# Order of the products inside a weight chunk: all products with the high part first, then those with the low part

## The chip, the cores and the metric

The kernel runs on one core of a Trainium2 chip (trn2). The metric is the device time of one execution in microseconds (us). It was run three times before the change; the median is 1704.13 us, the runs lie between 1700.52 and 1705.7. Of this kernel a difference of about 0.3% can be told from none.

## The reference

One inference step of a hybrid decoder layer (depth 1, model width 2048) for a prompt of 256 tokens and eight samples of one token each. The 264 tokens share the weights. Cut to what matters:

```python
z = x @ w_in                                   # 2048 x 13316, split among the mixers and four gates
A: forgetting attention, B: S5 state space, C: HGRN2, D: spatial-gating MLP      # four branches, 512 wide
m = sum_k sigmoid(gate_k) * (branch_k @ w_branch[k])
x = LN(alpha * x + m @ w_out)
gate, up = split(x @ w_ffn_up)                 # 2048 x 2*5632
x = LN(alpha * x + (silu(gate) * up) @ w_ffn_down)
```

Branch B needs, per group, an input matrix of 16 channels times 64 complex states. It is built from the parameters, transposed on TensorE and then used as the left operand for the state inputs. All outputs are fp32, with caches and states beside the two y tensors.

## The kernel before, in words

**A product of two fp32 numbers in three.** All big products are done in the type fp32r. To keep the precision of fp32, both operands are split into a high and a low part: `high = round(x)`, `low = x - high`. A product is then high weight times high operand, high weight times low operand and low weight times high operand, three matmuls that add up in PSUM. The right operand is 264 columns wide (256 prompt tokens and 8 samples; in the first four steps of the up projection 266). The output of one weight tile is 128 x 264 and lies in one PSUM bank.

**Chunks.** Weights come in chunks of 512 KB, 128 x 1024 numbers, that is eight tiles of 128 x 128: four k tiles (`kk`) times two column halves (`half`), and 24 products. Two halves go to two PSUM banks, and a pass of several chunks adds up in the same two. There are 540 chunks: 276 for w_in, w_branch, the S5 GLU and w_out (`chunk(n)`, L816 to L818) and 264 for the feed-forward layer (`products`, L1177 to L1179; the last chunk of all has a form of its own, `last_products`). In the feed-forward part the up projection has 22 steps of 8 chunks, of which the first four (with 266 columns) and the fifth are written out and the others are a hardware loop; the down projection has 8 passes of 11 chunks, written out.

**Who does what with a chunk.** SP loads it into a ring (five slots, later four). ACT writes its high part (`hi_done` or `hi2` goes up by one; L1290, L1586), DVE subtracts and writes the low part (`lo_done` or `lo2`; L1702, L2395), TensorE multiplies. DVE waits for ACT's high part, and TensorE waits for DVE's low part before the first of the 24 products. With the last product TensorE raises `used` (or `used2`), and by that ACT may write the slot again, SP may load it, and ACT or DVE may evacuate a finished pass.

**The order on TensorE.** The order of the work is written out by hand. `until(n)` issues all chunks up to number n, and the small products of the branches stand between such calls. Every engine runs its list in order and waits for semaphores only. ACT and DVE have lists of their own (`weights(n)`, `more()`), in which splits of chunks and the small work of the branches are interleaved.

**S5's matrix.** DVE builds `bd` in the middle of its first splits (L1888 to L1892) and then tells `s5_bd`; GpSimd builds the identity. TensorE transposes `bd` into banks 4 and 5 (`transposes("s5_bt", r, ...)`, L832, two times four). ACT copies the result into `bt` (L1364) and tells `s5_bt_ready`, for which TensorE waits after chunk 13 before the samples' products (L970). 

**Other places that come up.** L954 is a warm-up of six matmuls on a tile of ones ahead of the first chunk. Between chunks 54 and 62 L1021 broadcasts the values of one sample after each chunk, and DVE updates that sample's state from it (L2070). L839 sums over partitions with a matrix of ones (fp32). `hp` holds the operand of the down projection: for each k tile 264 high numbers, then 264 low ones 288 places further on; `x1p` holds that of the up projection in the same way.

Of the kernel before, what the change touches and what calls it, by code (L numbers as in the profile page):

```python
# [12 lines left out]
P = 128  # L13
# [4 lines left out]
TOK = SEQ + DEC  # L18
# [12 lines left out]
CK = 4  # L31
# [200 lines left out]
def trunk(nc, A, O):  # L232
# [551 lines left out]
    def _(pe):  # L784
        done = [FIRST]

        def chunk(n):
# [15 lines left out]
            if kind == "out":  # L803
                right_h, right_l = mh, ml
                if a == 0:
                    pe.wait_ge(sem("ml_done"), 2 * kc + 2)
            pe.wait_ge(sem("lo_done"), n - FIRST + 1)
            slot, tiles = n % RING, 1 if kind == "ff" else 2
            per = CK * 2 // tiles
            for kk in range(per):  # L810
                k = kc * per + kk
                first, last = k == 0, k == count * per - 1
                for half in range(tiles):
                    out = PS[:, BANK(p) + half, 0:TOK]
                    c = slice((kk * tiles + half) * P, (kk * tiles + half) * P + P)
                    nc.tensor.matmul(out, w_split[:, slot, 0, c], right_h[:, k, :], start=first, stop=False)  # L816
                    nc.tensor.matmul(out, w_split[:, slot, 0, c], right_l[:, k, :], start=False, stop=False)  # L817
                    ins = nc.tensor.matmul(out, w_split[:, slot, 1, c], right_h[:, k, :], start=False, stop=last)  # L818
            ins.then_inc(sem("used"), 1)

        def weights(upto):
# [131 lines left out]
        for _ in range(6):  # L953
            nc.tensor.matmul(PS[:, 7, :].rearrange("p (a t) -> p a t", a=4), ones[:, :],  # L954
                             ones[:, :].unsqueeze(1).to_broadcast([P, 4, P]), start=True, stop=True)
        until(11)
        pe.wait_ge(*told("ident_ready", 1))
        pe.wait_ge(*told("s5_bd", 1))
        for r in range(2):
# [207 lines left out]

        def products(slot, bank, right_h, right_l, k0, first, last, width=TOK):  # L1170

            for kk in range(CK):
                rh, rl = right_h(k0 + kk, width), right_l(k0 + kk, width)
                for half in range(2):
                    out = PS[:, bank + half, 0:width]
                    c = slice((kk * 2 + half) * P, (kk * 2 + half) * P + P)
                    nc.tensor.matmul(out, w_hi[:, slot, c], rh, start=(first and kk == 0), stop=False)  # L1177
                    nc.tensor.matmul(out, w_hi[:, slot, c], rl, start=False, stop=False)  # L1178
                    ins = nc.tensor.matmul(out, w_lo[:, slot, c], rh, start=False, stop=(last and kk == CK - 1))  # L1179
            ins.then_inc(sem("used2"), 1)  # L1180

# [24 lines left out]
        def up_chunk(i, j, right_h, right_l, width=TOK):  # L1206
            n, p, kc = C_UP + j, P_UP + j // 4, j % 4
            if kc == 0:
                pe.wait_ge(sem(f"evac{p % 2}"), i + p // 2)
            pe.wait_ge(sem("lo2"), i * 8 + (n + 1))  # L1210
            products(n % RING2, BANK(p), right_h, right_l, CK * kc, kc == 0, kc == 3, width)

        for i in range(Z_STEPS):
            for j in range(8):
# [16 lines left out]
        for m in range(8):  # L1231
            p = P_DOWN + m
            for kc in range(DOWN_CHUNKS):
                n = C_DOWN + m * DOWN_CHUNKS + kc
                if kc == 0:
                    pe.wait_ge(sem(f"evac{p % 2}"), p // 2)
                if m == 0:
                    pe.wait_ge(sem("hl_done"), CK * (kc + 1) // 2)
                pe.wait_ge(sem("lo2"), n + 1)
                if (m, kc) == (7, DOWN_CHUNKS - 1):  # L1240
                    last_products(n % RING2, BANK(p), h_high, h_low, CK * kc)
                else:
                    products(n % RING2, BANK(p), h_high, h_low, CK * kc, kc == 0, kc == DOWN_CHUNKS - 1)
                if (m, kc) == (4, 5):
                    layer_pivot(1)

# [1410 lines left out]
```

## Time and profile before

| what | before |
|---|---|
| median of three runs | 1704.13 us (1700.52 to 1705.7) |
| the profiled execution, its span | 1702.31 us, 1700.4 us |
| TensorE busy | 1689.7 us, 99% of the span, 13806 matmuls |
| weight loads busy | 1642.0 us, 97%, 13806 |
| DVE, ACT, GpSimd busy | 1076.0 us (63%), 798.1 us (47%), 142.3 us (8%) |
| granted TensorE clock, mean | 0.997 |

The span runs from the first to the last instruction of the profiled execution; the time of an execution has a little more around it. Each engine's busy time is a share of the span. Matmuls overlap in the profile, because one takes 280 ns or so from its start to its end and the next starts some 120 ns after it; a busy share of 99% therefore says that TensorE always had a product under way, and the distance between two starts says how fast it is.

### The profile page before, as it was taken

To read this page: it belongs to the slowest core of one execution; us is meant where nothing else is said; L and a number is where in the kernel's file an instruction comes from. 1 tells how busy PE (TensorE), PEld (TensorE's weight loads), DVE (VectorE), ACT (ScalarE), POOL (GpSimd) and SP (SyncE) were. 2 spreads that over 40 slices of the span, in tenths; PEclk is the share of its full clock that TensorE was granted. 3 is DMA by queue.
4 is the path that set the end of the run, shared out by engine and by line. 5 is a ranking of instruction groups with operands and counts; after the bars stand their busy time and mean duration, and the time that the engine had idled before them with its cause. 6 is when DMAs were issued, how large, how long until landed. Compare 5 with 4: busy or idle time off the path is not lost.

```text
span 1700.4 us, 33405 instructions
## 1 busy us (share of the span) xinstructions
PE 1689.7 (99%) x13806; PEld 1642.0 (97%) x13806; DVE 1076.0 (63%) x1275; ACT 798.1 (47%) x894; POOL 142.3 (8%) x148
## 2 busy tenths in 40 slices
PE   9999999999999999999999999999999999999998
PEld 8999998999999999999999999999999999999997
DVE  7888897766557666455688784444444444455655
ACT  5655544656444444444355563444434443333433
POOL 8200000000012555000000000000000000000000
PEclk9999999999999999999999999999999999999998
DMA  8566567776657888666556556656556565655652
GB/s 259 160 208 165 159 216 246 229 233 212 211 149 241 287 255 251 190 185 179 181 175 197 186 166 194 185 181 179 183 185 182 178 183 186 186 177 170 197 176 76
DMA packets 310582, 329.75 MB, mean 194 GB/s; under 512 B 12223, under 2 KB 292035, under 8 KB 310212
## 3 DMA queue, kind: packets, MB, share of 16 engines
q1 hardware_dynamic: 309068, 326.59, 62.7%
q8 instruction: 84, 1.38, 0.3%
q10 hardware_dynamic: 1400, 1.54, 0.3%
q14 instruction: 30, 0.25, 0.0%
HBM read 322.31 MB, written 5.77 MB: 193 GB/s over the span
## 4 chain that ended last, share of the span: by engine, by line
PE 98%; DVE 1%; DMA 0%; issue 0%; ACT 0%; SPq 0%; DVEq 0%
PE ps L816 16%; PE ps L817 16%; PE ps L818 16%; PE ps L1178 15%; PE ps L1177 15%; PE ps L1179 15%; PE ps L889 1%; PE ps L1066 1%; PE ps L924 1%; PE ps L854 0%; PE ps L832 0%; DMA w_in_ring<-in_w_in 0%; DVE w_split L1702 0%; PE ps L839 0%; PE ps L1269 0%; PE ps L867 0%
## 5 line engine op out<-in xcount | busy, mean ns | idle before, releaser
L2395 DVE TENSOR_TENSOR w_lo<-w_raw,w_hi 128x1024 fp32r<-128x1024 f32 x264 | 322.8, 1225 | 318.8 <-ACT w_hi L1586 315.8
L1702 DVE TENSOR_TENSOR w_split<-w_in_ring,w_split 128x1024 fp32r<-128x1024 f32 x276 | 351.2, 1276 | 234.3 <-ACT w_split L1290 224.3
L816 PE MATMUL ps<-xh,w_split 128*128 128x264 f32 x1680 | 481.2, 286 | 2.1 <-DVE w_split L1702 2.1
L1586 ACT ACTIVATE w_hi<-w_raw 128x1024 fp32r<-128x1024 f32 x264 | 279.8, 1061 | 429.8 <-PE ps L1179 425.0
L817 PE MATMUL ps<-xl,w_split 128*128 128x264 f32 x1680 | 477.9, 284 | 0.0
L818 PE MATMUL ps<-xh,w_split 128*128 128x264 f32 x1680 | 476.5, 284 | 0.0
L1290 ACT ACTIVATE w_split<-w_in_ring 128x1024 fp32r<-128x1024 f32 x276 | 291.2, 1059 | 352.1 <-DMA w_in_ring<-in_w_in 263.8
L1178 PE MATMUL ps<-x1p,w_hi 128*128 128x264 f32 (+1 forms) x1408 | 400.3, 284 | 0.0
L1177 PE MATMUL ps<-x1p,w_hi 128*128 128x264 f32 (+1 forms) x1408 | 399.0, 283 | 0.0
L1179 PE MATMUL ps<-x1p,w_lo 128*128 128x264 f32 (+1 forms) x1408 | 393.9, 280 | 0.0
L816 PEld LDWEIGHTS ps<-xh,w_split 128*128 128x128 f32 x1680 | 315.9, 188 | 18.1 <-issue 12.7
L817 PEld LDWEIGHTS ps<-xl,w_split 128*128 128x128 f32 x1680 | 315.9, 188 | 0.2
L818 PEld LDWEIGHTS ps<-xh,w_split 128*128 128x128 f32 x1680 | 315.9, 188 | 0.0
L1177 PEld LDWEIGHTS ps<-x1p,w_hi 128*128 128x128 f32 x1408 | 265.1, 188 | 0.0
L1179 PEld LDWEIGHTS ps<-x1p,w_lo 128*128 128x128 f32 x1408 | 265.0, 188 | 0.0
L1178 PEld LDWEIGHTS ps<-x1p,w_hi 128*128 128x128 f32 x1408 | 264.3, 188 | 0.0
L1178 PE MATMUL ps<-hp,w_hi 128*128 128x264 f32 x696 | 197.7, 284 | 0.0
L1177 PE MATMUL ps<-hp,w_hi 128*128 128x264 f32 x696 | 196.9, 283 | 0.0
L1179 PE MATMUL ps<-hp,w_lo 128*128 128x264 f32 x696 | 195.8, 281 | 0.0
L1177 PEld LDWEIGHTS ps<-hp,w_hi 128*128 128x128 f32 x696 | 130.9, 188 | 0.0
L1179 PEld LDWEIGHTS ps<-hp,w_lo 128*128 128x128 f32 x696 | 130.8, 188 | 0.0
L1178 PEld LDWEIGHTS ps<-hp,w_hi 128*128 128x128 f32 x696 | 130.7, 188 | 0.0
(499 smaller groups left out, 1787.6 us busy)
## 6 DMA issues: line engine op xcount, KB each, us to landing
w_in_ring<-in_w_in SPq DMA_DIRECT2D x210, 512.0 KB, 3.8
w_raw<-in_w_ffn_up SPq DMA_DIRECT2D x176, 512.0 KB, 4.1
w_raw<-in_w_ffn_down SPq DMA_DIRECT2D x88, 512.0 KB, 3.5
kv<-in_cache_k SPq DMA_DIRECT2D x64, 258.0 KB, 3.8
w_in_ring<-in_w_branch SPq DMA_DIRECT2D x32, 512.0 KB, 4.5
kv<-in_cache_v SPq DMA_DIRECT2D x64, 256.0 KB, 3.7
w_in_ring<-in_w_out SPq DMA_DIRECT2D x32, 512.0 KB, 3.4
x_t<-in_x SPq DMA_DIRECT2D x8, 264.0 KB, 7.0
```

Of the source, the lines that this page charges most:

```text
L816: nc.tensor.matmul(out, w_split[:, slot, 0, c], right_h[:, k, :], start=first, stop=False)
L817: nc.tensor.matmul(out, w_split[:, slot, 0, c], right_l[:, k, :], start=False, stop=False)
L818: ins = nc.tensor.matmul(out, w_split[:, slot, 1, c], right_h[:, k, :], start=False, stop=last)
L889: ins = nc.tensor.matmul(PS[32 * h:32 * h + DEC, bank, :].rearrange("p (a t) -> p a t", a=4), q_rows[:, h, b, :], kv[:, u % 2, :, h * P:h ...
L924: ins = nc.tensor.matmul(PS[32 * j:32 * j + 32, bank, :], ptt[:, 32 * (8 * b + 4 * half + j):32 * (8 * b + 4 * half + j) + 32], kv[:, u % ...
L1177: nc.tensor.matmul(out, w_hi[:, slot, c], rh, start=(first and kk == 0), stop=False)
L1178: nc.tensor.matmul(out, w_hi[:, slot, c], rl, start=False, stop=False)
L1179: ins = nc.tensor.matmul(out, w_lo[:, slot, c], rh, start=False, stop=(last and kk == CK - 1))
L1290: A_(w_split[:, n % RING, 0, :], w_in_ring[:, n % RING, 1, :], ACT.Copy).then_inc(sem("hi_done"), 1)
L1586: A_(w_hi[:, n % RING2, :], raw[:, n % RING2, :], ACT.Copy).then_inc(sem("hi2"), 1)
L1702: V.tensor_tensor(w_split[:, slot, 1, :], w_in_ring[:, slot, 1, :], w_split[:, slot, 0, :], ALU.subtract).then_inc(sem("lo_done"), 1)
L2395: V.tensor_tensor(w_lo[:, n % RING2, :], raw[:, n % RING2, :], w_hi[:, n % RING2, :], ALU.subtract).then_inc(sem("lo2"), 1)
```

## The change

Within a chunk the 24 products keep their operands, their banks and their number. Before, the three products of a weight tile came one after another. After, the 16 products with the high weights of all eight tiles come first, tile by tile (high operand, low operand), and then the eight with the low weights. TensorE waits for the high part before the 16 and for the low part before the eight. The first product of a pass starts its bank and the last low product ends it. The last chunk of all keeps its order and its wait. And the transposes of S5's matrix move from behind chunk 11 to behind chunk 12.

```diff
@@ chunk(n)
-            pe.wait_ge(sem("lo_done"), n - FIRST + 1)
+            pe.wait_ge(sem("hi_done"), n - FIRST + 1)
             for kk in range(per):
                 k = kc * per + kk
                 for half in range(tiles):
...
                     nc.tensor.matmul(out, w_split[:, slot, 0, c], right_h[:, k, :], start=(k == 0), stop=False)
                     nc.tensor.matmul(out, w_split[:, slot, 0, c], right_l[:, k, :], start=False, stop=False)
-                    ins = nc.tensor.matmul(out, w_split[:, slot, 1, c], right_h[:, k, :], start=False, stop=last)
+            pe.wait_ge(sem("lo_done"), n - FIRST + 1)
+            for kk in range(per):
+                k = kc * per + kk
+                for half in range(tiles):
...
+                    ins = nc.tensor.matmul(out, w_split[:, slot, 1, c], right_h[:, k, :], start=False,
+                                           stop=(k == count * per - 1))
             ins.then_inc(sem("used"), 1)
@@ before the transposes of s5_bt
-        until(11)
+        until(12)
@@ products(): the same, with the count of the chunk as an argument
+            pe.wait_ge(sem("hi2"), count)
             for kk in range(CK):
...
                     nc.tensor.matmul(out, w_hi[:, slot, c], rh, start=(first and kk == 0), stop=False)
                     nc.tensor.matmul(out, w_hi[:, slot, c], rl, start=False, stop=False)
+            pe.wait_ge(sem("lo2"), count)
+            for kk in range(CK):
+                rh = right_h(k0 + kk, width)
+                for half in range(2):
...
                     ins = nc.tensor.matmul(out, w_lo[:, slot, c], rh, start=False, stop=(last and kk == CK - 1))
             ins.then_inc(sem("used2"), 1)
@@ up_chunk, and the down loop in the same way; before last_products the wait for lo2 stays
-            pe.wait_ge(sem("lo2"), i * 8 + (n + 1))
-            products(n % RING2, BANK(p), right_h, right_l, CK * kc, kc == 0, kc == 3, width)
+            products(i * 8 + (n + 1), n % RING2, BANK(p), right_h, right_l, CK * kc, kc == 0, kc == 3, width)
```

## Rows read from the trace of the kernel before

**Rows 1.** Profile: busy us (share of span) xinstructions; last chain by engine.

```profile
PE 1689.7 (99%) x13806; PEld 1642.0 (97%) x13806; DVE 1076.0 (63%) x1275; ACT 798.1 (47%) x894; POOL 142.3 (8%) x148
...
PE 98%; DVE 1%; DMA 0%; issue 0%; ACT 0%; SPq 0%; DVEq 0%
```

**Rows 2.** Waits of TensorE's matmuls: total us, times, longest us.

```profile
PE ps L816 <- DVE w_split L1702: 2.1, 2, 1.8
PE ps L954 <- POOLq L252: 1.1, 1, 1.1
```

**Rows 3.** Windows: stretch, length, busy (count) by engine, granted clock, DMA.

```profile
720.00:820.00 100.00, 100.00 (x826) 100.00 (x825) 54.95 (x55) 44.19 (x49) 0.00 (x0) 1.00 0.63 182
1020.00:1420.00 400.00, 400.00 (x3336) 400.00 (x3335) 193.47 (x174) 165.26 (x175) 0.00 (x0) 1.00 0.60 183
1460.00:1560.00 100.00, 100.00 (x836) 100.00 (x835) 52.36 (x51) 36.82 (x35) 0.00 (x0) 1.00 0.58 180
1580.00:1660.00 80.00, 80.00 (x661) 80.00 (x660) 46.74 (x47) 32.48 (x34) 0.00 (x0) 1.00 0.61 189
940.00:1000.00 60.00, 60.00 (x489) 60.00 (x488) 47.71 (x64) 32.24 (x43) 0.00 (x0) 1.00 0.58 178
860.00:920.00 60.00, 60.00 (x493) 60.00 (x492) 49.55 (x72) 32.68 (x51) 0.00 (x0) 1.00 0.58 185
```

**Rows 4.** Timeline of TensorE at 1568.7 us: start, us, instruction.

```profile
1568.86 0.61 PE L839 MATMUL ps<-acc_d,ones 128*128 128x264 f32 x2
```

**Rows 5.** Timeline of the first chunk's start; in brackets: idle, releaser.

```profile
7.96 1.02 PE L954 MATMUL ps<-ones 128*128 128x512 f32 x2
8.30 1.06 ACT L1290 ACTIVATE w_split<-w_in_ring 128x1024 fp32r<-128x1024 f32 x1 [3.20 <-DMA w_in_ring<-in_w_in]
9.39 1.22 DVE L1702 TENSOR_TENSOR w_split<-w_in_ring,w_split 128x1024 fp32r<-128x1024 f32 x1 [3.55 <-ACT w_split L1290]
...
10.76 0.36 PE L816 MATMUL ps<-xh,w_split 128*128 128x264 f32 x1 [1.78 <-DVE w_split L1702]
```

**Rows 6.** Timeline of weight loads and DVE's splits, 186 to 217 us.

```profile
186.41 0.19 PEld L1021 LDWEIGHTS ps<-t,pick 72*128 72x128 f32 x1
189.64 0.19 PEld L1021 LDWEIGHTS ps<-t,pick 72*128 72x128 f32 x1
192.80 0.19 PEld L1021 LDWEIGHTS ps<-t,pick 72*128 72x128 f32 x1
202.14 1.22 DVE L1702 TENSOR_TENSOR w_split<-w_in_ring,w_split 128x1024 fp32r<-128x1024 f32 x1
203.42 0.19 PEld L816 LDWEIGHTS ps<-xh,w_split 128*128 128x128 f32 x1 [0.21 <-DVE w_split L1702]
206.32 0.19 PEld L1021 LDWEIGHTS ps<-t,pick 72*128 72x128 f32 x1
215.37 1.22 DVE L1702 TENSOR_TENSOR w_split<-w_in_ring,w_split 128x1024 fp32r<-128x1024 f32 x1
216.44 0.19 PEld L818 LDWEIGHTS ps<-bh,w_split 128*128 128x128 f32 x1
216.71 0.19 PEld L816 LDWEIGHTS ps<-xh,w_split 128*128 128x128 f32 x1
```

**Rows 7.** Timeline around S5's transposes, 41 to 50 us.

```profile
41.37 0.87 DVE L1892 TENSOR_TENSOR bd<-tmp 64x256 f32<-64x256 f32 x2
41.71 1.06 ACT L1290 ACTIVATE w_split<-w_in_ring 128x1024 fp32r<-128x1024 f32 x1 [2.48 <-DMA w_in_ring<-in_w_in]
42.39 1.23 DVE L1702 TENSOR_TENSOR w_split<-w_in_ring,w_split 128x1024 fp32r<-128x1024 f32 x1 [0.15 <-DVE bd L1892]
42.95 1.03 PE L832 MATMUL ps<-ident,bd 128*128 128x128 f32 x8
48.14 1.31 ACT L1364 ACTIVATE bt<-ps 128x512 f32<-128x512 f32 x2
49.77 0.63 PE L970 MATMUL ps<-su,bt 32*128 32x8 f32 x16
```

More of the change, by code:

```diff
@@ L811, in chunk @@
                 k = kc * per + kk
-                first, last = k == 0, k == count * per - 1
                 for half in range(tiles):
@@ L815, in chunk @@
                     c = slice((kk * tiles + half) * P, (kk * tiles + half) * P + P)
-                    nc.tensor.matmul(out, w_split[:, slot, 0, c], right_h[:, k, :], start=first, stop=False)
+                    nc.tensor.matmul(out, w_split[:, slot, 0, c], right_h[:, k, :], start=(k == 0), stop=False)
                     nc.tensor.matmul(out, w_split[:, slot, 0, c], right_l[:, k, :], start=False, stop=False)
-                    ins = nc.tensor.matmul(out, w_split[:, slot, 1, c], right_h[:, k, :], start=False, stop=last)
+            pe.wait_ge(sem("lo_done"), n - FIRST + 1)
+            for kk in range(per):
+                k = kc * per + kk
+                for half in range(tiles):
+                    out = PS[:, BANK(p) + half, 0:TOK]
+                    c = slice((kk * tiles + half) * P, (kk * tiles + half) * P + P)
+                    ins = nc.tensor.matmul(out, w_split[:, slot, 1, c], right_h[:, k, :], start=False,
+                                           stop=(k == count * per - 1))
             ins.then_inc(sem("used"), 1)
@@ L1166, in _, with products @@
         until(END - 1)
-        def products(slot, bank, right_h, right_l, k0, first, last, width=TOK):
+        def products(count, slot, bank, right_h, right_l, k0, first, last, width=TOK):
+            pe.wait_ge(sem("hi2"), count)
             for kk in range(CK):
@@ L1178, in products @@
                     nc.tensor.matmul(out, w_hi[:, slot, c], rl, start=False, stop=False)
+            pe.wait_ge(sem("lo2"), count)
+            for kk in range(CK):
+                rh = right_h(k0 + kk, width)
+                for half in range(2):
+                    out = PS[:, bank + half, 0:width]
+                    c = slice((kk * 2 + half) * P, (kk * 2 + half) * P + P)
                     ins = nc.tensor.matmul(out, w_lo[:, slot, c], rh, start=False, stop=(last and kk == CK - 1))
@@ L1238, in _ @@
                     pe.wait_ge(sem("hl_done"), CK * (kc + 1) // 2)
-                pe.wait_ge(sem("lo2"), n + 1)
                 if (m, kc) == (7, DOWN_CHUNKS - 1):
+                    pe.wait_ge(sem("lo2"), n + 1)
                     last_products(n % RING2, BANK(p), h_high, h_low, CK * kc)
                 else:
-                    products(n % RING2, BANK(p), h_high, h_low, CK * kc, kc == 0, kc == DOWN_CHUNKS - 1)
+                    products(n + 1, n % RING2, BANK(p), h_high, h_low, CK * kc, kc == 0, kc == DOWN_CHUNKS - 1)
                 if (m, kc) == (4, 5):
```

## The prediction

> **What bounds the kernel now.** I read the head of the page first: the span is 1700.4 us, TensorE is busy for 99% of it, and 98% of the chain that ended last is its matmuls [rows 1]. The profiled execution took 1702.31 us, 1.9 more than its span; the median shown is 1704.13, so I work out a difference on the span and take it off the median. Next I read the list of waits: in the whole execution TensorE's matmuls waited for a low part (DVE, L1702) twice, 2.1 us in all, 1.8 of it before the first chunk, and they waited for no low part of the second ring [rows 2]. So the change moves waits on the right engine, but waits that hardly exist. Last I read windows over six stretches with nothing but weight products in them, because 540 chunks of 24 products are what TensorE's time is made of: what one product takes there is worth more than all waits together.
>
> **The pace of a product.** A window counts an instruction that it only cuts; matmuls of 0.28 us that follow each other every 0.12 add about 2.35. So 400 us with 3336 counted are 400/3333.65 = 120.0 ns for one product, in the up phase; 1460:1560 gives 120.0 in the first half of the down phase; 1580:1660 gives 80/658.65 = 121.5 in its second half; 720:820 gives 121.4 in the first weights; 860:920 gives 122.3 in the output projection; 940:1000 gives 123.3 in the first four up steps, where the right operand is two columns wider [rows 3]. The granted clock is 1.00 in all six, the level of 2.4 GHz, so the clock doesn't make the difference. Nor does the shape: the down phase runs 120.0 and then 121.5 with the same instructions on the same tile hp, and what stands between is one short interruption, the two fp32 sums of L839 [rows 4]. So this engine's pace isn't fixed by columns alone. It falls into one steady rhythm or another, and which one depends on what was read before. The change keeps every product and every operand but puts them in another order: a rhythm is what it can upset.
>
> **What goes: the start.** The first chunk's high part is ready at 8.30 + 1.06 = 9.36 us, the low part at 9.39 + 1.22 = 10.61, and the first product starts at 10.76, 0.15 later [rows 5]. After the change it waits for the high part only: 9.36 + 0.15 = 9.51. The low part is wanted after 16 products, 16 x 0.1214 = 1.94 us later, at 11.45, when it has long been there. Gain 1.25 us. The warm-up matmuls end at 7.96 + 1.02 = 8.98, so they aren't in the way.
>
> **What goes: the stretch where DVE is late.** Between 186 and 206 us DVE works off eight sample states between its splits. TensorE's L1021 (four of its seven rows are shown) stands behind each chunk there and comes seven times from 186.41 to 206.32: 19.91 us in six steps. The shortest step is 3.16 (189.64 to 192.80); six of them are 18.96, so 0.95 us were lost. At 216.44 the step to the next weight load is 0.27 in place of 0.12, 0.15 more [rows 6]. With the low part wanted 1.94 us later these go. But TensorE now comes 1.25 us earlier and DVE, busy with its own queue here, doesn't. The split that ends at 202.14 + 1.22 = 203.36 belongs to the chunk that started at 203.42; that chunk would now start at 203.42 - 1.25 - 0.95 = 201.22 and want it at 203.16: 0.20 late, 0.25 with the delay of a semaphore. The one that ends at 215.37 + 1.22 = 216.59 is wanted at about 216.71 - 1.25 - 0.95 - 0.15 + 0.25 + 1.94 = 216.55: 0.05 late, 0.1 with the delay. So 1.10 - 0.35 = 0.75 us stay.
>
> **What moves: the S5 transposes.** They need bd, which DVE finishes at 41.37 + 0.87 = 42.24. Before, they start at 42.95, after chunk 11. With TensorE 1.25 earlier they would come at 41.70 and wait 0.55; behind chunk 12, which takes 24 x 0.1214 = 2.91, they come at about 44.6 and don't. Chunk 12 itself then starts at 41.7 and wants its low part at 43.6; DVE finishes it at 42.39 + 1.23 = 43.62, just in time, at worst 0.15 late with the delay. The eight transposes issue no DMA and pass nothing but chunk 12 in TensorE's queue; SP and GpSimd wait for none of them. Their readers: ACT copies bt at 48.14, late for other reasons, and TensorE's L970 wants the copies (ready at 48.14 + 1.31 = 49.45) at 49.77 [rows 7]. TensorE comes there 1.25 earlier, at 48.5. ACT's queue up to that point hangs on a weight chunk at 41.71, for which it sat idle 2.48 us, and that transfer is issued when TensorE gives a slot back, so it moves with TensorE. I take 0. If ACT stays where it is, 1.0 of the 1.25 is lost here.
>
> **What is added.** One more wait in each of 539 chunks. Behind it stand the chunk's eight low products and then all that TensorE has queued; ACT (who reuses w_hi), SP (who reloads the slot) and the evacuations wait for the last of the eight, as before, and that is still the chunk's last product. A wait that is already met costs nothing that can be seen: in the 400 us of the up phase there are 139 of them and a product still takes 120.0 [rows 3]; the rounding of that pace, 0.04 ns a product, leaves 1 ns a chunk, 0.5 us in all, as the upper end. ACT's split takes 1.06 us and DVE's 1.22 [rows 5] of the 2.9 of a chunk; neither becomes the bound. The sum: -1.25 - 0.75 = -2.0 us. Its bounds are -2.4 (nothing is late) and +0.5 (DVE and ACT take all of it back, and the waits cost their upper end).
>
> **The pace after it.** No row shows the new order, so I bound it by the paces that the rows do show. A chunk had the right operands high, low, high for each weight tile; now it has high, low sixteen times in turn, then high eight times. How often a high follows a high, a low a high and a high a low is eight times a chunk in both orders, and every product still has its own weight load. That speaks for the same pace, and I take a change of 0. The bounds: 4656 products run at 120.0 now (3456 of the later up steps, 1200 of the first down chunks). At 121.5 they cost +7.0 us, at the 123.3 of the wider steps +15.4. Downwards, the 5856 products of the first weights at 120.0 in place of 121.4 to 121.5 give -8.5; the 768 of the output projection, the 768 wider ones and the 912 of the late down phase give -1.8, -2.5 and -1.4 more.
>
> The rows say that the same product takes 120.0 or 121.5 ns. The Trainium skill (SBUF — State Buffer, Who interferes with whom) gives TensorE two read ports of its own and says it waits for no one; and "TensorE: Matmul & The Clock Gate", Back-to-back issue gap, puts an isolated matmul at its columns over 2.4 GHz and 2.5 ns, which for 264 columns is 112.5 ns, an estimate from that page. By these the order can't matter to the pace, and the time is the sum of the waits alone; by the rows it can, since two stretches with one shape differ. The measurement decides, so the rivals below keep their chances.
>
> **The forecast and the rivals.** About 5 us, 0.3%, is what a measurement here can tell from no change: faster is under 1699.0, slower over 1709.2.
>
> *The waits go and the pace stays* (0.40): 1704.1 - 2.0 = 1702.1; its own range is 1699.5 to 1705.5. For it: the equal counts of neighbours; against it: the two paces of one tile.
>
> *The start is not kept* (0.05): ACT's copies of bt or DVE's states hand the lead back: 1703.5 to 1704.5.
>
> *The rhythm of the later phases is lost* (0.30), the one that ends on the other side. Place: the up steps from 1010 us and the first 50 down chunks, where a product takes 120.0. Eight high operands in a row, or the change from pairs to singles once a chunk, throw it into the rhythm that the second half of the down phase already has. Price 7.0 us, less 2.0: 1709.1; if the first weights also go to the 122.3 of the output projection, 0.9 x 5856 = 5.3 more, 1714. It decides for slower as soon as all 4656 lose 1.5 ns. For it: one interruption was enough to lose the rhythm for good [rows 4]. About 0.07 of the 0.30 stays within 0.3%.
>
> *The first weights find the rhythm* (0.25): high and low in strict turn is a simpler pattern than before. 1704.1 - 2.0 - 8.5 = 1693.6; with every slow stretch, 1688. Against it: four stretches out of six don't have it now. About 0.02 of this stays within 0.3%.
>
> So faster 0.23, same 0.40 + 0.05 + 0.07 + 0.02 = 0.54, slower 0.23. The range reaches from 1691 (most of the last case) to 1712 (most of the third).
>
> **What would show it.** The first product at 9.5 us; no PE wait for a low part in the list, or only ones of 0.3 around 203 and 216; L832 at 44 to 45 us with no idle before it, L970 at about 48.5. The windows in the same stretches tell the rest: 120.0 in the up phase keeps the forecast, 121.5 there makes it wrong to the slow side, and under 121 in the first weights makes it wrong to the fast side. A new TensorE wait for ACT's high parts would make it wrong in a way that I gave no chance.

## The result

The change makes the kernel faster: 1689.45 us (median of six runs, 1688.39 to 1691.82) against 1702.81 for the kernel before in the same session (six runs, 1700.11 to 1705.7). The ratio is 0.9927, its 95% interval 0.9916 to 0.9938. The forecast was 1702.1, "same" in the sense of within 0.3%, with a range down to 1691; all three were wrong. Of the runs reported below one, a tenth run of e2_in_only, took 6881.47 us and is left out of that kernel's interval.

The profiled execution of after took 1688.39 us with a span of 1686.6, 13.8 less than the span before. The lines of after that answer to [rows 1 to 7] follow; line numbers have moved (L954 is L960, L1021 is L1027, L1179 is L1192).

The head and the chain, as in [rows 1]. TensorE is the bound as before, and has 13.2 us less to do with the same 13806 instructions:

```profile
PE 1676.5 (99%) x13806; PEld 1630.5 (97%) x13806; DVE 1078.4 (64%) x1275; ACT 798.3 (47%) x894; POOL 142.2 (8%) x148
...
PE 97%; DMA 1%; POOL 1%; DVE 1%; ACT 0%; issue 0%; SPq 0%; DVEq 0%; POOLq 0%; ACTq 0%
```

All waits of TensorE's matmuls (total us, times, longest), as in [rows 2]. The wait for low parts is gone, and two new ones stand there:

```profile
PE ps L960 <- POOLq L252: 1.1, 1, 1.1
PE ps L815 <- ACT gate L1322: 0.8, 1, 0.8
PE ps L1151 <- DVEq L252: 0.7, 1, 0.7
```

The windows, as in [rows 3], cut to where each stage now lies. A count holds about 2.4 matmuls that the window only cuts, so the pace is the length over the count less 2.4:

```profile
720.00:800.00 80.00, 80.00 (x661) 80.00 (x660) 43.50 (x44) 35.66 (x39) 0.00 (x0) 1.00 0.63 179
1020.00:1400.00 380.00, 380.00 (x3214) 380.00 (x3213) 186.23 (x168) 159.24 (x167) 0.00 (x0) 1.00 0.60 186
1460.00:1550.00 90.00, 90.00 (x762) 90.00 (x762) 46.18 (x46) 33.96 (x32) 0.00 (x0) 1.00 0.57 183
1570.00:1650.00 80.00, 80.00 (x679) 80.00 (x678) 47.97 (x49) 33.45 (x34) 0.00 (x0) 1.00 0.61 194
940.00:1000.00 60.00, 60.00 (x488) 60.00 (x487) 47.70 (x65) 32.43 (x43) 0.00 (x0) 1.00 0.58 178
860.00:910.00 50.00, 50.00 (x412) 50.00 (x411) 40.38 (x58) 25.52 (x37) 0.00 (x0) 1.00 0.59 191
```

Here is the gain. In the up phase from step 4 on (second line) a product takes 380/3211.6 = 118.3 ns, where it took 120.0. Both halves of the down phase (third and fourth) run at 118.5 and 118.2, where they ran at 120.0 and 121.5; by the starts of the chunks both are at 118.3. The other three stand at 121.5, 123.6 and 122.1: within half a ns of before.

The matmul L845, which answers to [rows 4], still interrupts the down phase; now the same pace goes on behind it:

```profile
1559.72 0.61 PE L845 MATMUL ps<-acc_d,ones 128*128 128x264 f32 x2
```

The pace inside one chunk of the up phase (timeline of TensorE: start, us, instruction):

```profile
1200.92 1.12 PE L1192 MATMUL ps<-x1p,w_lo 128*128 128x264 f32 x8
1201.88 0.28 PE L1184 MATMUL ps<-x1p,w_hi 128*128 128x264 f32 x1
1202.00 0.28 PE L1185 MATMUL ps<-x1p,w_hi 128*128 128x264 f32 x1
1202.12 0.28 PE L1184 MATMUL ps<-x1p,w_hi 128*128 128x264 f32 x1
...
1203.76 0.64 PE L1192 MATMUL ps<-x1p,w_lo 128*128 128x264 f32 x4
```

The eight low products take 1201.88 - 1200.92 = 0.96 us, 120 ns each. The first two high ones take 0.24, 120 each. The other fourteen take 1.64 (1202.12 to 1203.76), 117. By the start times of all chunks of these steps, 15 of a chunk's 24 distances are at 116.7 on the mean, and a chunk takes 2840 ns where it took 2880.

The start, as in [rows 5], and the sample states, as in [rows 6] (first and last of seven weight loads):

```profile
7.34 1.06 ACT L1302 ACTIVATE w_split<-w_in_ring 128x1024 fp32r<-128x1024 f32 x1 [2.21 <-DMA w_in_ring<-in_w_in]
8.60 0.19 PEld L815 LDWEIGHTS ps<-xh,w_split 128*128 128x128 f32 x1 [0.24 <-issue]
8.63 0.69 PE L815 MATMUL ps<-xh,w_split 128*128 128x264 f32 x1
...
184.64 0.19 PEld L1027 LDWEIGHTS ps<-t,pick 72*128 72x128 f32 x1
...
203.56 0.19 PEld L1027 LDWEIGHTS ps<-t,pick 72*128 72x128 f32 x1
```

S5's transposes, as in [rows 7]:

```profile
40.76 0.87 DVE L1904 TENSOR_TENSOR bd<-tmp 64x256 f32<-64x256 f32 x2
44.14 1.04 PE L838 MATMUL ps<-ident,bd 128*128 128x128 f32 x8
45.68 1.31 ACT L1376 ACTIVATE bt<-ps 128x512 f32<-128x512 f32 x2
48.04 1.97 PE L976 MATMUL ps<-su,bt 32*128 32x8 f32 x64
```

Where the 13.8 us of span went, by the starts of the stages in the two traces: the first product starts 2.1 earlier (10.76 to 8.63), and of the lead 1.4 is left where up step 4 begins (1010.1 to 1008.7). Up steps 4 to 21 take 414.7 before and 409.0 after, the first 50 down chunks 144.25 and 142.25, the last 38 110.9 and 108.1: together 10.5. The tail behind the last product takes 20.4 before and 18.5 after: 1.9. That tail difference isn't the change's. Before, the engine's rows double in length at its end; after, they don't:

```profile
1687.76 1.15 PE L1269 MATMUL ps<-mu_r,minus 1*128 1x264 f32 x4
1688.84 2.13 PE L1266 MATMUL ps<-yp,ident 128*128 128x264 f32 x4
1690.90 2.12 PE L1269 MATMUL ps<-mu_r,minus 1*128 1x264 f32 x4
```

```profile
1676.91 1.16 PE L1278 MATMUL ps<-yp,ident 128*128 128x264 f32 x4
1678.00 1.15 PE L1281 MATMUL ps<-mu_r,minus 1*128 1x264 f32 x4
```

Windows of the two ends (the third number from the right is the granted clock) show the cause, before and then after:

```profile
1688.00:1700.30 12.30, 5.02 (x12) 2.76 (x11) 6.98 (x11) 6.37 (x13) 0.00 (x0) 0.53 0.50 176
```

```profile
1676.00:1686.50 10.50, 3.15 (x12) 1.83 (x12) 7.05 (x11) 6.32 (x13) 0.00 (x0) 0.64 0.58 206
```

Before, the clock is at its lower level, 1.2 GHz, while the last two rows run, and these take 2.13 us in place of 1.16; after, it falls only when they are done. When the clock falls differs between executions, in kernels with the change and without: with it the profiled tails run from 18.5 us (after, where the clock falls 11.0 behind the last product of the last chunk) to 22.5 (e7_low272, 6.5 behind it), without it they are 20.4 (before, 8.9 behind it) and 18.5 (e18_before_turn, 13.2 behind it).

### The profile page after: what moved, and what is told of

The parts are those of the page before. It is cut to its first block, busy times and chain, and to the rows that moved or that the text cites. A ratio compares the mean times of both kernels' runs of the same rounds, so it can differ in the third digit from the quotient of the medians.

```text
span 1686.6 us, 33405 instructions
## 1 busy us (share of the span) xinstructions
PE 1676.5 (99%) x13806; PEld 1630.5 (97%) x13806; DVE 1078.4 (64%) x1275; ACT 798.3 (47%) x894; POOL 142.2 (8%) x148
## 4 chain that ended last, share of the span: by engine, by line
PE 97%; DMA 1%; POOL 1%; DVE 1%; ACT 0%; issue 0%; SPq 0%; DVEq 0%; POOLq 0%; ACTq 0%
PE ps L815 15%; PE ps L823 15%; PE ps L1192 15%; PE ps L816 15%; PE ps L1185 15%; PE ps L1184 15%; PE ps L895 1%; PE ps L1072 1%; DMA w_in_ring<-in_w_in 1%; PE ps L860 1%; PE ps L960 0%; PE ps L838 0%; PE ps L930 0%; POOL v_sum L779 0%; PE ps L845 0%; PE ps L873 0%
## 5 line engine op out<-in xcount | busy, mean ns | idle before, releaser
L815 PE MATMUL ps<-xh,w_split 128*128 128x264 f32 x1680 | 421.7, 287 | 0.8 <-ACT gate L1322 0.8
L816 PE MATMUL ps<-xl,w_split 128*128 128x264 f32 x1680 | 416.3, 283 | 0.0
L1184 PE MATMUL ps<-x1p,w_hi 128*128 128x264 f32 (+1 forms) x1408 | 341.3, 280 | 0.0
L1185 PE MATMUL ps<-x1p,w_hi 128*128 128x264 f32 (+1 forms) x1408 | 340.6, 280 | 0.0
L815 PEld LDWEIGHTS ps<-xh,w_split 128*128 128x128 f32 x1680 | 315.9, 188 | 15.5 <-issue 12.7
L823 PE MATMUL ps<-xh,w_split 128*128 128x264 f32 x1680 | 238.8, 284 | 0.0
L823 PEld LDWEIGHTS ps<-xh,w_split 128*128 128x128 f32 x1680 | 218.2, 188 | 0.1
L1192 PE MATMUL ps<-x1p,w_lo 128*128 128x264 f32 (+1 forms) x1408 | 198.9, 283 | 0.0
L1192 PEld LDWEIGHTS ps<-x1p,w_lo 128*128 128x128 f32 x1408 | 181.6, 188 | 0.0
L1184 PE MATMUL ps<-hp,w_hi 128*128 128x264 f32 x696 | 167.4, 279 | 0.0
L1185 PE MATMUL ps<-hp,w_hi 128*128 128x264 f32 x696 | 166.8, 279 | 0.0
L1192 PE MATMUL ps<-hp,w_lo 128*128 128x264 f32 x696 | 97.8, 283 | 0.0
L1192 PEld LDWEIGHTS ps<-hp,w_lo 128*128 128x128 f32 x696 | 89.2, 188 | 0.0
```

## The experiments

One window, 1020 to 1400 us, lies inside up steps 4 to 21 in every kernel. It is shown for each; the pace is 380 us over the count less 2.4 (after: x3214, 118.3 ns). Kernels are compared by this pace first, because single times also differ by the tail: 18.5 us in after, 21.9 in e6_half_major and 22.0 in e17_cross_mended. Edits are shown against after, or against the kernel that the text names, and cut to the feed-forward where both parts of the kernel get the same.

### The change in parts

**e1_ff_only.** Only `products()` has the new order; `chunk()` and the transposes are as before.

```diff
-            pe.wait_ge(sem("hi_done"), n - FIRST + 1)
+            pe.wait_ge(sem("lo_done"), n - FIRST + 1)
...
-        until(12)
+        until(11)
```

> Only the feed-forward chunks have the new order; the chunks of w_in, w_branch and w_out and the place of the S5 transposes are those of before. Theory (the order of the right operands sets the pace: high and low in strict turn run at 116.7 ns a product, a high behind a high at about 121): a product in the late up steps takes 118.3 ns as after the change, the first weights 121.5; the whole is 10.5 us under before, up to 12.4 if the end's slow clock is missed too, 1690 to 1693. Rival (the earlier start and the waits gave the gain): the start and the stretch at 186 to 206 us wait as before, so at most 1 us is gained, 1702.

1691.3 us (four runs), ratio 0.9945 (0.9928 to 0.9962).

```profile
1020.00:1400.00 380.00, 380.00 (x3214) 380.00 (x3213) 186.69 (x168) 158.74 (x167) 0.00 (x0) 1.00 0.60 186
```

118.3 ns with the feed-forward's order alone, and most of the gain with it.

**e2_in_only.** The counterpart: `chunk()` and the transposes new, `products()` as before.

```diff
-            pe.wait_ge(sem("hi2"), count)
...
-            pe.wait_ge(sem("lo2"), count)
-            for kk in range(CK):
...
+            pe.wait_ge(sem("lo2"), i * 8 + (n + 1))
...
```

> Only the chunks of w_in, w_branch and w_out have the new order, and the S5 transposes stand behind chunk 12; the feed-forward chunks are those of before. Theory of the operands' order: late up steps back at 120.0 ns, first weights at 121.5 as in both kernels; what is left is the waits, 1.4 to 2 us under before, 1700.8 to 1701.5. Rival (waits): nearly the whole gain, 1690 to 1692.

1699.53 us (median of ten runs), ratio 0.9986 (0.9976 to 0.9996).

```profile
1020.00:1400.00 380.00, 380.00 (x3169) 380.00 (x3169) 183.19 (x165) 156.95 (x166) 0.00 (x0) 1.00 0.59 183
```

Back to 120.0. What is left, 1699.5 against 1702.6 (0.7 to 4.1 us by the interval), is the part that the forecast was about: the waits.

**e3_one_wait.** The new order, but the wait for the low part stands at the head of the chunk.

```diff
-            pe.wait_ge(sem("hi2"), count)
+            pe.wait_ge(sem("lo2"), count)
...
-            pe.wait_ge(sem("lo2"), count)
```

> The new order everywhere, but one wait ahead of each chunk, for the low part, as before the change. Theory of the operands' order: late up steps stay at 118.3 ns; the first product comes 1.25 us later again and the stretch at 186 to 206 us loses 0.9: 1.4 to 2 us over the changed kernel, 1690.8 to 1691.5. Rival (waits): back to 1702.

1693.19 us (four runs, 1690.29 to 1695.86, over the 1690.8 to 1691.5 expected), ratio 0.9955 (0.9938 to 0.9972); `chunk()` is changed likewise.

```profile
1020.00:1400.00 380.00, 380.00 (x3214) 380.00 (x3213) 186.74 (x168) 158.76 (x168) 0.00 (x0) 1.00 0.60 186
```

The order makes the pace, not the later wait.

**e14_s5_at_11.** Only the transposes go back to chunk 11.

```diff
-        until(12)
+        until(11)
```

> The changed kernel with S5's matrix transposed at chunk 11 again, as before the change: the third part of the change alone, undone. Theory 'the move is worth nothing' (the prediction's step): the first weights' phase starts and ends as in the changed kernel within 1 us, span 1685 to 1690 us. Rival 'the move takes away a wait at the start': the products up to chunk 16 end 1 us or more later against their own start.

1688.4 us, span 1686.6, as after. TensorE does wait there (timeline; in brackets the idle time before and its releaser), but up step 4 starts at 1008.69 us, in after at 1008.73: what the move saves at 42 us is given back before that.

```profile
41.97 1.06 PE L838 MATMUL ps<-ident,bd 128*128 128x128 f32 x8 [0.79 <-DVEq L252]
```

### What in the order makes the pace

The first theory was that products with operands in turn are short, that is, a product whose right operand is the other one (low after high, high after low) than that of the product before it.

**e5_cross.** Operands in turn in the 16 high products, but no weight tile twice in a row.

```diff
+            for turn_ in range(2):
+                for tile in range(2 * CK):
...
+                    right = (right_h, right_l)[(tile + turn_) % 2](k0 + kk, width)
```

> The changed kernel, but among the 16 high-weight products no weight tile comes twice in a row and each product changes the PSUM bank: tile 0 with the high operand, tile 1 with the low, tile 2 with the high, and so on, then the same tiles with the other operand. High and low operands are still in strict turn. Theory of the operands' order: late up steps stay at 118.3 ns within 0.4, 1689 to 1691. Rival (the pair of products with the same weights, or two products on one bank, makes the gain): the 16 lose their 116.7, the steps go to 120 or 121, 1697 to 1706.

1708.9 us, slower than before.

```profile
1020.00:1400.00 380.00, 380.00 (x3133) 380.00 (x3132) 181.92 (x164) 155.22 (x164) 0.00 (x0) 1.00 0.58 182
```

121.4 ns. I took the theory to have fallen, and asked whether pairs (two products in a row with one weight tile) or the PSUM bank make the difference. That was a misreading of my own edit, as e17_cross_mended shows.

**e6_half_major.** The changed order with the bank kept for eight products (four in the low part).

```diff
-            for kk in range(CK):
...
-                for half in range(2):
+            for half in range(2):
+                for kk in range(CK):
```

> In both parts of a chunk the loop over the two halves (the two PSUM banks) goes outside the loop over k: pairs with one weight tile stay, and the bank now stays the same for eight products, also in the low part (four there), where the changed kernel switches it at each product. Theory 'pair' (one weight tile twice in a row with the operand going from high to low makes the short pitch): high part stays at about 116.7 ns a product, low part at about 121, so 118.3 ns in up 4-21 and down, span 1686 to 1690 us. Rival 'bank' (a product that goes on in the bank of the one before it is short): the low part falls to about 116.7 as well, 2800 ns a chunk in place of 2840, 40 ns x 232 chunks = 9 us less, span about 1677 to 1680.

```profile
1020.00:1400.00 380.00, 380.00 (x3214) 380.00 (x3213) 186.43 (x168) 159.08 (x167) 0.00 (x0) 1.00 0.60 186
```

1692.85 us; 118.3 as in after, chunk for chunk 2840 ns. The bank has no part in it.

**e11_cross_bank.** e5_cross with the half outside.

```diff
-                for tile in range(2 * CK):
+                for half, kk in [(half, kk) for half in range(2) for kk in range(CK)]:
...
-                    right = (right_h, right_l)[(tile + turn_) % 2](k0 + kk, width)
+                    right = (right_h, right_l)[(kk + turn_) % 2](k0 + kk, width)
```

> As e5_cross (operands in strict turn, no weight tile twice in a row), but the half goes outside, so four products in a row go on in one bank. Rival 'turn and bank' (operands in turn are enough where the bank stays): about 118.3 ns a product in up 4-21 and down, as in the changed kernel, span 1686 to 1690 us. Theory 'pair' (one weight tile twice in a row is needed): about 121.4 as in e5_cross, span 1704 to 1708.

```profile
1020.00:1400.00 380.00, 380.00 (x3133) 380.00 (x3132) 181.87 (x164) 154.96 (x163) 0.00 (x0) 1.00 0.58 181
```

1709.95 us, 121.4 again.

**e12_pairs_turned.** Pairs again, but high low, low high, so every second one of the 16 high products repeats the operand.

```diff
+                    pair = [rh, rl] if half == 0 else [rl, rh]
...
```

> As the changed kernel, but with half 1 the low operand comes before the high one (high low, low high, ...): each weight tile is still used twice in a row in one bank, but from one tile to the next the operand stays the high or the low one. Rival 'weights alone' (the second use of a weight tile is short, whatever the operand): 118.3 ns in up 4-21 and down, span 1686 to 1690 us. Theory 'pair in turn' (the operand has to change at each product as well): 120 ns or more there, span 1695 to 1705.

```profile
1020.00:1400.00 380.00, 380.00 (x3133) 380.00 (x3132) 181.42 (x164) 155.97 (x164) 0.00 (x0) 1.00 0.58 181
```

1711.42 us, 121.4: pairs alone do not give 118.3, the operand must turn.

**e17_cross_mended.** In e5_cross the two rounds over the tiles meet with the low operand twice. In its first chunk of up step 4 the starts are 117, 117, 116, 117, 117, 116 ns apart up to that place, then 120, 124, 121. In the chunks behind it the first half isn't short either (121, 123, 121, 128, 121, 119, 118, 117 in the third), although its operands still turn there. Here that one repeat is taken out, by the second round taking the tiles in the order 1, 0, 3, 2 and so on.

```diff
-                for tile in range(2 * CK):
+                for i_ in range(2 * CK):
+                    tile = i_ ^ turn_
...
-                    right = (right_h, right_l)[(tile + turn_) % 2](k0 + kk, width)
+                    right = (right_h, right_l)[i_ % 2](k0 + kk, width)
```

> e5_cross mended: there the two rounds over the high weights' tiles met with the low operand twice in a row (product 8 to 9 of a chunk, and its trace leaves the short pitch at that place), so its operands did not turn at every one of the 16 products. Here the second round takes the tiles 1, 0, 3, 2, ... so that high and low operand strictly take turns over all 16; no weight tile serves twice in a row, the low part is all high operands as in the changed kernel. Theory 'turn alone' (pairs have no part; e5_cross lost the pitch by its one repeat): the pitch is found again within the 16 products and held to their end, between 2840 and 2880 ns a chunk, 118.3 to 120.0 ns on the mean in up 4-21 and down, span 1686 to 1696 us. Rival 'pairs lead back in after a low part without turns': not found, 121 to 122 ns, span 1702 to 1709.

```profile
1020.00:1400.00 380.00, 380.00 (x3214) 380.00 (x3213) 186.76 (x168) 158.87 (x167) 0.00 (x0) 1.00 0.60 186
```

1693.97 us, 118.3, without a single pair. So with these places turning is what counts; one repeat in the middle of 16 cost 3 ns for each of the chunk's 24 products.

### What "in turn" means: the operand's place

**e7_low272.** The order of after; only the place of the low operand changes, by 64 bytes.

```diff
-PAIR, LOW = 576, 288
+PAIR, LOW = 576, 272
```

> The changed kernel with the low operand of each feed-forward tile 272 places (1088 bytes) behind the high one, not 288 (1152 bytes); order, weights and arithmetic unchanged. Rival 'order alone' (the place of the operands has no part in it): 118.3 ns in up 4-21 and down, span 1686 to 1690 us. Theory 'place' (the high and the low operand have to start 128 bytes apart within 256): 120 ns or more in up 4-21 and down, span 1695 to 1706.

```profile
1020.00:1400.00 380.00, 380.00 (x3119) 380.00 (x3118) 180.79 (x163) 154.66 (x163) 0.00 (x0) 1.00 0.58 180
```

1713.32 us, 121.9, the worst of all. So it isn't enough that high and low turn: where they start counts. By the kernel's own offsets (HH_PHASE, X1_PLACES), taken modulo 256 bytes, the high operands start at byte 192; the low ones, 288 x 4 = 1152 bytes on, at 64. Here they start at 0.

**e9_in_turn.** The first weights get the same: a chunk takes k tiles kc, kc+4, kc+8, kc+12, high and low 128 bytes apart, low first at every other k tile.

```diff
-                k = kc * per + kk
+                k = kc + 4 * kk if apart else kc * per + kk
+                pair = [right_h, right_l]
+                if apart and kk % 2:
+                    pair.reverse()
...
-    xh = place("xh", [P, KT, TOK], F32R, at_xh + XW - XB)
+    xh = place("xh", [P, KT, TOK], F32R, at_xh)
```

> The changed kernel with the operands of the first weights re-laid so that the three conditions hold there too: a chunk of w_in and w_out takes the k tiles kc, kc+4, kc+8, kc+12 (whose high operands lie 128 bytes apart within 256, in turn), the low operands lie 128 bytes from the high ones, and for every other k tile the low operand comes first; 228 of the 276 chunks there, the arithmetic the same but for the order of sums. Theory 'pair, turn and place': the 16 high products of these chunks fall from 121.5 to about 116.7 ns, the 8 low ones stay at about 121, 118.3 on the mean: 3.2 ns x 24 x 228 = 17 us less where no other wait takes it, so a span of about 1669 to 1676 us, and the feed-forward at 118.3 as before. Rival 'feed-forward only' (the pace of the first weights is set by something else, VectorE or the transfers): 121 to 122 ns there, span 1684 to 1691.

1687.83 us, ratio 0.991 (0.9891 to 0.9929). Windows of four chunks of the output projection one after another, kc = 3, 0, 1, 2:

```profile
849.84:852.79 2.95, 2.95 (x26) 2.95 (x25) 2.65 (x4) 1.01 (x1) 0.00 (x0) 1.00 0.65 149
852.79:855.71 2.92, 2.92 (x27) 2.92 (x26) 2.70 (x5) 0.67 (x2) 0.00 (x0) 1.00 0.73 186
855.71:858.66 2.95, 2.95 (x26) 2.95 (x25) 2.73 (x5) 2.44 (x6) 0.00 (x0) 1.00 0.74 183
858.66:861.51 2.85, 2.85 (x27) 2.85 (x25) 2.71 (x4) 2.51 (x6) 0.00 (x0) 1.00 0.79 177
```

Neither side was right. In after the k tiles of such a chunk follow one another, 1056 bytes apart, so the places move on by 32 bytes modulo 256 with each. Here, by the offsets, all 24 products of a chunk turn between two places: 128 and 0 (kc = 0), 160 and 32 (1), 192 and 64 (2), 224 and 96 (3). By the starts of all re-laid chunks that nothing interrupts, those with kc = 2 are the short ones (117.8 to 119.1 ns a product); kc = 0 stays at 121.5 to 121.8 and kc = 3 at 122.2 in w_in and 123.1 in the output projection. In the projection kc = 2 is short with 2.71 us of VectorE work and 177 GB/s, kc = 1 isn't with 2.73 and 183, so these loads don't set its pace.

The chunks kc = 1 come at two paces with one order and the same places: 12 at 120.0, the others at 122.9 to 123.5. Two of them, both of the gates:

```profile
250.31:253.19 2.88, 2.88 (x27) 2.88 (x26) 2.85 (x5) 0.01 (x1) 0.00 (x0) 1.00 0.95 318
284.10:287.06 2.96, 2.96 (x26) 2.96 (x25) 1.66 (x4) 1.06 (x1) 0.47 (x1) 1.00 0.59 161
```

So even a strict turn in a chunk doesn't settle its pace at these places. What decides between these two wasn't looked for; the shorter one is the one with the higher load here.

**e8_ff_turn.** The feed-forward's operands in rows of 288, so that the next k tile lies 128 bytes further on modulo 256 and the low products turn as well.

```diff
+    hh = place("hh", [P, D_FF // P, ROW], F32R, at_hh)[:, :, 0:TOK]
+    hl = place("hl", [P, D_FF // P, ROW], F32R, at_hh + (D_FF // P) * ROW * 4 + 128)[:, :, 0:TOK]
...
+                if kk % 2:
+                    pair.reverse()
...
-            for kk in range(CK):
-                rh = right_h(k0 + kk, width)
-                for half in range(2):
+            for half in range(2):
+                for kk in range(CK):
+                    rh = right_h(k0 + kk, width)
```

> The changed kernel with the feed-forward's operands re-laid so that they turn by 128 bytes at every product of a chunk, in the low part too (rows of 288 places, so neighbours in k lie 128 bytes apart; low operand first at odd k; low part with the half outside). In the low part each weight tile still serves once. Theory 'pair, turn and place, all three': the low part stays at about 121 ns, 118.3 on the mean, span 1685 to 1690 us. Rival 'turn and place are enough in a run that is already in the rhythm': the low part falls to about 116.7, 2800 ns a chunk, 116.7 on the mean, span 1676 to 1680.

```profile
1020.00:1400.00 380.00, 380.00 (x3260) 380.00 (x3259) 188.47 (x170) 161.95 (x170) 0.00 (x0) 1.00 0.60 189
```

1680.71 us in its one run. 116.7 ns, 2800 a chunk: my theory of three conditions (pair, turn and place) was wrong on this one, the rival right. The low part needs no pairs.

**e15_no_pairs.** The same places, all eight tiles with the high operand, then all eight with the low.

```diff
-                    nc.tensor.matmul(out, w_hi[:, slot, c], pair[0], start=(first and kk == 0), stop=False)
-                    nc.tensor.matmul(out, w_hi[:, slot, c], pair[1], start=False, stop=False)
+            for right, order in ((right_h, (0, 1, 2, 3)), (right_l, (1, 0, 3, 2))):
...
```

> e8_ff_turn without pairs: in the feed-forward all eight products of the high weights with the high operand come first, then the eight with the low operand, then the low weights, so that operands still turn by 128 bytes at every product and no weight tile serves twice in a row anywhere. Theory 'pairs only lead back in' (a chunk that always turns keeps the short pitch by itself once it has it; without any pair it may never find it) has two readings: if turn and place are the whole condition, 116.7 ns in up 4-21 and down, span about 1679 to 1683 us. Rival 'pairs are needed': 121 to 121.5 ns there, as in e5_cross and e11_cross_bank, span 1703 to 1709.

```profile
1020.00:1400.00 380.00, 380.00 (x3259) 380.00 (x3258) 188.42 (x170) 161.97 (x170) 0.00 (x0) 1.00 0.60 189
```

1680.93 us, 116.7.

**e16_places_0_128.** e8_ff_turn with every operand 64 bytes lower.

```diff
-HH_PHASE = 192
+HH_PHASE = 128
...
-    x1_groups = [(place(f"x1h{g}", [P, CK, ROW], F32R, at_x1 + g * X1_GROUP + 192),
+    x1_groups = [(place(f"x1h{g}", [P, CK, ROW], F32R, at_x1 + g * X1_GROUP + 128),
```

> e8_ff_turn with all operands of the feed-forward 64 bytes lower: they start at 128 and 0 bytes of 256 in place of 192 and 64, still 128 bytes apart in turn; the order is the same. Theory 'the place itself counts' (from e9_in_turn, where chunks at 128 and 0 stayed at 121.7 ns and those at 192 and 64 fell to 118.0 to 118.4): 121 to 122 ns in up 4-21 and down, span 1703 to 1710 us. Rival 'only the distance counts': 116.7 ns, span about 1679 to 1683.

```profile
1020.00:1400.00 380.00, 380.00 (x3126) 380.00 (x3125) 180.97 (x163) 154.50 (x163) 0.00 (x0) 1.00 0.57 180
```

1704.83 us, 121.7. So the distance of 128 bytes isn't enough either: the places 64 and 192 themselves count.

### What is best, and whether the change is needed

**e10_both.** e8_ff_turn and e9_in_turn together.

```diff
+            apart = spread(n)
...
+    hh = place("hh", [P, D_FF // P, ROW], F32R, at_hh)[:, :, 0:TOK]
```

> e8_ff_turn and e9_in_turn together: the feed-forward's operands turn at every product, and a quarter of the chunks of w_in and w_out lie at 64 and 192 bytes of 256. If the two savings add: e8_ff_turn 7.6 us under the changed kernel by its span, and e9_in_turn 1.5 us at the start of the feed-forward (1007.00 against 1008.43 in e8_ff_turn), so a span of about 1677 us, a time of about 1679, ratio to before about 0.986. If e8_ff_turn's low part needs no more than its own order: 116.67 ns in up 4-21 and down again.

1680.29 us (four runs), ratio to before 0.9871 (0.9855 to 0.9888). The span of the profiled execution is 1676.2, so there the two savings add (1679.0 for e8_ff_turn, 1686.2 for e9_in_turn, 1686.6 for after); the four times, 1678.13 to 1681.98, don't tell it from e8_ff_turn's 1680.71.

**e18_before_turn.** The kernel before, its order of three products a tile and its one wait; only the places of e8_ff_turn and the half as the outer loop.

```diff
-            for kk in range(CK):
...
-                for half in range(2):
+            for half in range(2):
+                for kk in range(CK):
...
+    hh = place("hh", [P, D_FF // P, ROW], F32R, at_hh)[:, :, 0:TOK]
```

> The kernel before with nothing of the change (three products of a weight tile one after another, one wait, S5 at chunk 11), but with the feed-forward's operands re-laid as in e8_ff_turn and the half as the outer loop, so that high, low, high of one tile and then low-lying, high-lying, low-lying of the next turn between 192 and 64 bytes of 256 at every product. Theory 'turn of the place is the whole condition': 116.7 ns in up 4-21 and down although the order is the old one, span about 1681 to 1685 us (1700.4 less 19 for the pace, tail and start as they fall), ratio about 0.990. Rival 'the order by weights has a part of its own (products of the high weights in one run)': 120 ns or more there, span 1699 to 1703.

```profile
1020.00:1400.00 380.00, 380.00 (x3259) 380.00 (x3259) 189.47 (x171) 161.93 (x170) 0.00 (x0) 1.00 0.62 189
```

1681.04 us (four runs), ratio 0.9861 (0.9844 to 0.9877), 116.7 ns. Nothing of the change is in it, and it is ahead of both kernels: its interval lies wholly under that of after (0.9916 to 0.9938). With these places the order by weights has no part of its own. What it brought at the old places is how it lays the repeats of a place: eight together, where before each stood apart. Between this kernel and e10_both the intervals overlap.

## Why the prediction was wrong

**The step that failed** is "How often a high follows a high, a low a high and a high a low is eight times a chunk in both orders ... That speaks for the same pace, and I take a change of 0". The counts are right and the inference isn't. What the runs show to matter is not how many products repeat the place of the one before, but how they lie. Before, every third one repeats it (high, low, high, then high), and no chunk ever has a long run in turn: 360 ns for three, 120.0. After, eight repeats stand together. By the starts the eight distances from the second low product to the next chunk's second product are at 120.9 ns on the mean, the one behind them is 122.6, and the other 15 are at 116.7. e17_cross_mended and e15_no_pairs show that this needs no pairs, e6_half_major that it doesn't hang on the bank. The term set to 0 measures 5.7 + 2.0 + 2.8 = -10.5 us.

**The bound that failed with it.** Downwards the text let stages fall to 120.0, because that was the lowest pace in a row of before. 120.0 was itself a mixture, of a chunk 2880 ns long; 116.7 is reached where every product turns. The rival "the first weights find the rhythm" had nearly the right size, 1693.6 to 1688, by luck, since it was in the wrong place: those weights stayed at 121.5, and the feed-forward moved. The rival on the slow side wasn't absurd: e5_cross, e12_pairs_turned and e7_low272 are such kernels, one edit away, at 1709 to 1713.

**What held.** The sentence that the pace "falls into one steady rhythm or another" fits more than the row it came from. Before, the order and the places are the same in the whole down phase, and yet a chunk takes 2880 ns ahead of the interruption [rows 4] and 2910 to 2921 behind it. In after and in e8_ff_turn the second chunk behind it is back at 2840 and 2800. So of the 2.8 us that the change gains there about 1.3 are that loss undone, an estimate from 37 chunks at some 35 ns; the rest is the lower pace.

The Trainium skill (SBUF — State Buffer, Who interferes with whom) has TensorE wait for no one else, and nothing here speaks against that: the other engines do the same work in e8_ff_turn and e16_places_0_128. But from it the prediction went on to an order that can't matter, and the page doesn't say that; the operand's own place costs up to 121.9 against 116.7 ns. The isolated gap by the Trainium skill ("TensorE: Matmul & The Clock Gate", Back-to-back issue gap), 112.5 ns by estimate, is reached in no run: the lowest pace is 116.7.

**The start** was right in kind: TensorE's first product comes 0.23 behind ACT's split (8.40 to 8.63), where before it came 1.40 behind (9.36 to 10.76): 1.17, forecast 1.25. The other 0.96 of the 2.13 is the split itself, at 7.34 in place of 8.30, since its transfer landed earlier in that execution. **The sample states** gave 203.56 - 184.64 = 18.92 in place of 19.91, 0.99 where 0.95 was forecast, and the 0.35 of new delay in that stretch didn't come. **S5**: L838 came at 44.14 (forecast 44.6) with nothing late, L976 at 48.04 (48.5); the 0 holds (e14_s5_at_11). **The added waits** cost nothing that shows: e3_one_wait, without them, takes 2840 ns a chunk as after does with them.

**What the waits brought in all** is 1.4 us at step 4, forecast 2.0; in e2_in_only, another execution of the same first part, it is 2.5 (1010.1 to 1007.7). By the starts of the chunks the lead had grown to 3.1 us at 560 us. Then two things came too late for a TensorE that was ahead: 0.83 for L815 at 581.6, held up by ACT's `gate`, and 0.72 for L1151 at 611.4. Neither stood in [rows 2], and the prediction looked for late work only near the start and in the sample states.

**What stays open.** Why places 64 and 192 are short and others aren't, why one repeat costs a whole chunk, and why one order at one place has two paces (before's down phase, kc = 1 in e9_in_turn); no run looks inside the engine. That 256 bytes are the period is a way of writing the offsets and wasn't tested. Nor was it tried to bring all chunks of w_in to these places, which takes 96 bytes more for each of 32 operand tiles. What sets the pace of the first four up steps, 266 columns wide (123.3 even in e8_ff_turn, against 116.7 at 264), wasn't tested alone.

## What to carry to other kernels

Where TensorE bounds a kernel, first take the distance between two products from windows without interruptions: 116.7 to 121.9 ns for one shape is 4%, more than every wait in this profile together. Where stages with one shape run at different paces, work out at which byte (modulo 256 here) each product's right operand starts, product by product; a row of the trace shows the pace, and only the layout shows the places. The counts of neighbours aren't enough: ask whether the pattern runs through the chunk without a break. And read the pace on both sides of an interruption, since one order can come out of it slower.

## What the hardware showed that was not expected

The pace of fp32r products of 128 x 264 at the 2.4 GHz level depends on where the right operands start and in which order: 116.67 ns where starts turn between 64 and 192 modulo 256 at every product, 121.67 with 128 and 0, 121.9 with 192 and 0 in the order of after. In the later up steps it is the same from chunk to chunk within 1 ns: 2800 in e8_ff_turn, 2840 in after, 2880 before, 2914 in e5_cross, 2920 in e16_places_0_128, 2927 in e7_low272. Order and place within a chunk don't always settle it: before's chunks went from 2880 ns to between 2910 and 2921 behind one interruption, and the chunks kc = 1 of e9_in_turn took 120.0 ns a product or about 123.2. And the tail, with little for TensorE to do, takes 18.5 to 22.5 us, the longer the sooner its clock falls to the 1.2 GHz level (from 11 us behind the last product on 18.5, at 8.9 20.4, at 6.5 22.5).
